# Sparse attention of one decoder layer: four head pairs written out, doubled buffers, the softmax division on GpSimd

## What is computed

```python
logits = jnp.einsum('bqhd,bqkhd->bhqk', q, k_sel).astype(jnp.float32) * (HEAD_DIM ** -0.5)
logits = jnp.where(valid[:, None], logits, -jnp.inf)
p = jax.nn.softmax(logits, axis=-1)
return jnp.einsum('bhqk,bqkhd->bqhd', p.astype(v.dtype), v_sel)
```

## Time and profile before

| | us |
|---|---|
| median of 3 runs (2573.61 to 2583.09) | 2574.93 |
| the profiled execution | 2575.35 |
| its span in the trace | 2573.7 |
| `sparse`, first q transpose to the last copy of o (1081.3 to 1255.6) | 174.3 |

### The profile page before, as it was taken

One profiled execution on the slowest core, in us unless ns is written; L12 is line 12 of the kernel. 1 busy time (PEld: TensorE's weight loads), 2 busy tenths in 40 slices (PEclk: granted clock), 3 DMA queues, 4 the chain that ended last, 5 costly groups with the idle time before them and its releaser, 6 DMA issues. The chain is left out here.

```text
span 2573.7 us, 37913 instructions
## 1 busy us (share of the span) xinstructions
PE 2251.4 (87%) x13113; PEld 1818.4 (71%) x13113; DVE 1382.0 (54%) x2547; ACT 804.6 (31%) x1357; POOL 138.7 (5%) x226
## 2 busy tenths in 40 slices
PE   4877799999997888788578789979999999999995
PEld 3823588888884445455346567869999999999994
DVE  4416878565563442275334454434566656665566
ACT  4026210211215656566333342212222122212212
POOL 0000000000002443200100000000000000000000
PEclk9988899999998989999789989989999999999998
DMA  3212123223212110211399962202111011101102
GB/s 129 78 34 52 61 84 113 82 82 114 82 47 57 36 35 15 56 37 53 84 312 388 349 199 107 99 5 65 50 49 46 27 49 49 49 25 49 49 16 85
DMA packets 187163, 218.57 MB, mean 85 GB/s; under 512 B 28924, under 2 KB 120956, under 8 KB 185916
## 3 DMA queue, kind: packets, MB, share of 16 engines
q1 hardware_dynamic: 178740, 214.03, 25.2%
q10 hardware_dynamic: 8072, 3.05, 0.6%
q0 software_dynamic: 256, 0.27, 0.1%
HBM read 181.17 MB, written 36.13 MB: 84 GB/s over the span
## 5 line engine op out<-in xcount | busy, mean ns | idle before, releaser
L2417 DVE TENSOR_TENSOR x_all<-x_all,ff_down 128x512 f32<-128x512 f32 x396 | 272.2, 687 | 163.4 <-PE ff_down L2321 158.7
L2306 PE MATMUL ff_up<-m_hi,ff_up_hi 128*128 128x368 f32 x1056 | 348.4, 330 | 7.5 <-DVE ff_up_lo L2394 7.5
L2307 PE MATMUL ff_up<-m_lo,ff_up_hi 128*128 128x368 f32 x1056 | 348.8, 330 | 0.0
L2308 PE MATMUL ff_up<-m_hi,ff_up_lo 128*128 128x368 f32 x1056 | 348.2, 330 | 0.0
L411 PE MATMUL pr_acc<-pr_w_hi,h_hi 128*128 128x512 f32 x720 | 281.5, 391 | 16.2 <-DVE pr_w_lo L352 16.2
L412 PE MATMUL pr_acc<-pr_w_lo,h_hi 128*128 128x512 f32 x720 | 281.2, 391 | 0.0
L413 PE MATMUL pr_acc<-pr_w_hi,h_lo 128*128 128x512 f32 x720 | 281.0, 390 | 0.0
L827 DVE TENSOR_SCALAR_CACHE_REDUCE bi_flags<-scores,bi_thr 128x384 bf16<-128x384 f32 (+6 forms) x252 | 235.5, 992 | 1.3
L2306 PEld LDWEIGHTS ff_up<-m_hi,ff_up_hi 128*128 128x128 f32 x1056 | 198.8, 188 | 8.8 <-DVE ff_up_lo L2394 7.9
L2307 PEld LDWEIGHTS ff_up<-m_lo,ff_up_hi 128*128 128x128 f32 x1056 | 198.9, 188 | 0.9
L2308 PEld LDWEIGHTS ff_up<-m_hi,ff_up_lo 128*128 128x128 f32 x1056 | 198.8, 188 | 0.0
(11 more groups left out here) (289 smaller groups left out, 3801.4 us busy)
## 6 DMA issues: line engine op xcount, KB each, us to landing
out_proj<-pr_staged SPq DMA_DIRECT2D x90, 256.0 KB, 2.0
up_raw<-in_w_up SPq DMA_DIRECT2D x44, 512.0 KB, 5.0
w_raw<-in_w_in SPq DMA_DIRECT2D x10, 2048.0 KB, 7.9
sa_keys<-in_cache_k_a SPq DMA_DIRECT2D x64, 256.0 KB, 4.2
sa_keys<-in_cache_k_b SPq DMA_DIRECT2D x64, 256.0 KB, 7.7
sa_values<-in_cache_v_a SPq DMA_DIRECT2D x64, 256.0 KB, 7.5
sa_values<-in_cache_v_b SPq DMA_DIRECT2D x64, 256.0 KB, 5.3
ff_down_raw<-in_w_down SPq DMA_DIRECT2D x22, 512.0 KB, 3.5
```

The lines of the kernel that those rows point to most:

```text
L2306: pe.matmul(up[n][:], w, hi[:, c, at], start=c == 0, stop=False)
L2307: pe.matmul(up[n][:], w, lo[:, c, at], start=False, stop=False)
L2308: ins = pe.matmul(up[n][:], w_rest, hi[:, c, at], start=False, stop=c == KC - 1)
L2417: dve.tensor_tensor(at, at, down[n][:], ALU.add).then_inc(down_added.sem, 1)
```

## The change

`sparse` is written anew, and everything else is left as it is.

- The loop over pairs is gone: the instructions of all four pairs are written out, and the pipeline runs over g = 0..35, the 36 tiles of all pairs. All waits are on constants.
- `q_t`, `k_t`, `v_rows` and `o_all` are doubled, `prob` and its small companions have four buffers instead of three.
- The q/k batches of pair i+1 are made while pair i runs: batches 0 and 1 in step t = 6, batches 2 and 3 in step 7, batch 4 in step 8 (`QK_WITH`). They share the ring of four banks with the scores.
- The lags grow: turn(g) runs in step g+3 instead of g+2, use(g) in step g+4 instead of g+3, the copy of o in g+5.
- The division's two multiplications move from DVE to GpSimd. The reciprocal stays on DVE.

```diff
-    NS, NTB, R = 4, 2, 3
+    NS, NTB, R, TURN_LAG, USE_LAG = 4, 2, 4, 3, 4
+    NG = PAIRS * NT
+    QK_WITH = {6: (0, 1), 7: (2, 3), 8: (4,)}
...
-    q_rows, k_rows, v_rows = sb("q_rows", [P, NT, P]), sb("k_rows", [P, NT, P]), sb("v_rows", [P, NT, P])
-    q_t, k_t = sb("q_t", [P, ROWS]), sb("k_t", [P, ROWS])
+    v_rows = [sb(f"v_rows{b}", [P, NT, P]) for b in range(2)]
+    q_t = [sb(f"q_t{b}", [P, ROWS]) for b in range(2)]
+    k_t = [sb(f"k_t{b}", [P, ROWS]) for b in range(2)]
...
+        @block.gpsimd
+        def _(pool):
+            for g in range(NG):
+                r, w = tile_rows(g % NT), key_width(g % NT)
+                pool.wait_ge(parted, g + 1)
+                for hh in range(2):
+                    x = prob[g % R][hh][0:r, 0:w]
+                    pool.tensor_scalar(x, x, part[g % R][0:r, hh:hh + 1], None, ALU.mult).then_inc(shared, 1)
...
+            for b in range(len(QK)):
+                turn_qk(0, b)
+            for n in range(NG + USE_LAG):
+                if n < NG:
+                    score(n)
+                    i, t = divmod(n, NT)
+                    for b in QK_WITH.get(t, ()) if i + 1 < PAIRS else ():
+                        turn_qk(i + 1, b)
+                if TURN_LAG <= n < NG + TURN_LAG:
+                    turn(n - TURN_LAG)
+                if n >= USE_LAG:
+                    use(n - USE_LAG)
...
+            for n in range(NG + TURN_LAG):
+                if n < NG:
+                    i, t = divmod(n, NT)
+                    for b in QK_WITH.get(t, ()) if i + 1 < PAIRS else ():
+                        take_qk(i + 1, b)
+                if 1 <= n <= NG:
+                    power(n - 1)
+                if n >= TURN_LAG:
+                    take_turns(n - TURN_LAG)
...
-                        for hh in range(2):
-                            x = prob[t % R][hh][0:r, 0:w]
-                            dve.tensor_scalar(x, x, part[t % R][0:r, hh:hh + 1], None, ALU.mult).then_inc(shared.sem, 1)
...
+            for n in range(NG + USE_LAG + 1):
+                if n < NG:
+                    mask(n)
+                if 1 <= n <= NG:
+                    invert(n - 1)
+                if n >= USE_LAG + 1:
+                    evacuate(n - USE_LAG - 1)
```

More of the change, by code:

```diff
@@ L1348, in turn, with turn_qk @@
-            def turn(i, t):
-                r = tile_rows(t)
-                for c in turns_of[t]:
+            def turn_qk(i, b):
+                what, t0, n = QK[b]
+                c = copies_of[i, b]
+                if b == 0:
+                    pe.wait_ge(qk_in, 32 * (i + 1))
+                wait_taken(pe, c - NS)
+                for t in range(t0, t0 + n):
+                    for k, rows in enumerate([q_rows, k_rows] if what == "both" else [q_rows if what == "q" else k_rows]):
+                        at = (t - t0 + k) * P
+                        ins = pe.transpose(banks[c % NS][:, at:at + P], rows[:, t, :], ident[:])
+                ins.then_inc(made, 1)
@@ new lines, in score @@
+            def score(g):
+                i, t = divmod(g, NT)
+                if t == 0:
+                    pe.wait_ge(qk_out, by_act[copies_of[i, len(QK) - 1]])
+                for c, hh, k, a, w in scores_of[g]:
+                    if hh == 0:
+                        wait_taken(pe, c - NS)
+                        wait_taken(pe, c + 1 - NS)
+                    pe.matmul(banks[c % NS][:, 0:w], q_t[i % 2][half(hh), t * P:(t + 1) * P],
+                              k_t[i % 2][half(hh), a:a + w], start=True, stop=True).then_inc(made, 1)
@@ new lines, in use @@
+                        ins = pe.matmul(o[g % 2][half(hh), 0:r], v_rows[i % 2][0:w, kt, half(hh)],
+                                        prob_t[g % 2][hh][0:w, kt, 0:r], start=kt == 0, stop=kt == t)
+                ins.then_inc(used, 1)
+            for b in range(len(QK)):
+                turn_qk(0, b)
[9 more added lines that the diff above has]
+                    use(n - USE_LAG)
@@ new lines, in invert, with evacuate @@
+            def invert(g):
+                r = tile_rows(g % NT)
+                dve.wait_ge(powered, 2 * g + 2)
+                if g >= R:
+                    dve.wait_ge(shared, 2 * (g - R + 1))
+                dve.reciprocal(part[g % R][0:r, :], total[g % R][0:r, :]).then_inc(parted, 1)
+            def evacuate(g):
+                i, t = divmod(g, NT)
+                dve.wait_ge(used, g + 1)
+                if t == 0 and i >= 2:
+                    dve.wait_ge(stored[i % 2], 16 * (i // 2))
+                r = tile_rows(t)
+                dve.tensor_copy(o_all[i % 2][:, t * P:t * P + r], o[g % 2][:, 0:r]).then_inc(o_out, 1)
```

264 lines of the change are left out of this document (115 added, 149 removed).

## The result

The changed kernel takes 2590.05 us, the median of five runs (2584.68 to 2593.09). The kernel before took 2574.93 us beside it, also five runs (2573.61 to 2583.09). The ratio is 1.0052, with a 95% interval of 1.0032 to 1.0073. On a second chip, against 11 runs of the kernel before, six more runs gave 1.0046 (1.0032 to 1.0059). So the change makes the kernel slower by about half a per cent: 12 to 13 us by the ratios, 15 us by the medians of the first measurement. The profiled execution is the one of 2590.05 us, 14.7 us above the profiled execution of before.

A forecast was written before the change was run, and what follows sets the result against it. PE was taken as the bound, busy 87% of the span, so only its 26.8 us of idle time in the stage could be won. 2575.35 + 3.4 (idle) + 3.5 (clock) gave 2582 us, range 2564 to 2596.

The forecast's parts named there:

- Idle time: PE's idle time in the stage: 24 us for three handovers plus 6.2 us elsewhere, 30.2 us against 26.8 before.
- steps 7, 8 and 9: Pipeline steps at each handover between pairs, where PE would stand still for 3.0, 3.0 and 1.35 us behind ACT.
- the small steps: Steps 3 to 5 of a pair, where tiles are small; 1 us of PE idle time was forecast there.
- ACT's chain of 4.6 us: In step 7, from batch 2's start on PE: two q/k copies 1.78, two exponentials 2.06, hand-off 0.74 us.
- the 0.93 us for two batches: PE's work on batches 2 and 3 in step 7, which with five transposes of 0.7 us fills part of the wait.
- The clock: PE's clock falls in every second of six stalls, 3 x 1.7 us, less 1.6 at the old seam: +3.5 us.
- The rival with a fall in every stall: The clock falls in every stall and stays low longer, 5 us, costing 2.5 us each: 2592 us; chance 0.20.
- The period: Time from pair to pair in the stage: about 44 us, against 42.6 before.
- GpSimd's price: The division's multiplications on GpSimd: 1.6 us for 1024 elements; up to 3.8 ns an element nothing waits, 0 in the sum.
- DVE's relief: The division leaves DVE, about 9 us less per pair, from 28 to some 19 us; alone worth little.
- DVE beside POOL: GpSimd's work holding up DVE's operations in the stage: 0 us.
- The covered rival: ACT finishes the exponential before PE's third group, handovers cost nothing, the stage falls to 156 us: 2557 us; chance 0.09.

The follow-up runs named there:

- e4_filler: The changed kernel with 16 repeated transposes in the second group of turn(4) and turn(5) of the first three pairs, filling PE's stalls; ratio 1.0045 to the kernel before.
- e1_act_order: The changed kernel with ACT's exponential of tile n-1 ahead of the q/k batch copies of step n; 2574.15 us, ratio 0.9984 to the kernel before.
- e2_div_vector: The changed kernel with the division's two multiplications back on DVE, right behind the reciprocal; ratio 1.0073 to the kernel before.
- e3_both: The changed kernel with the exponential ahead of the q/k copies on ACT and the division back on DVE; ratio 1.0003 to the kernel before.
- e10_between_div_vector: e8_use_between with the division back on DVE; ratio 0.9976 to the kernel before.
- e8_use_between: e1_act_order with PE's products of tile n-4 put between the second and third group of turn(n-3); 2561.91 us, ratio 0.9936 to the kernel before.
- e11_lag_two: e1_act_order with the short lags of before (turns 2 steps behind the scores, products 3), division on GpSimd; ratio 1.0060 to the kernel before.

## Why the prediction was right, and where it was wrong

The forecast was 2582 us; it came to 2590, inside the range. The direction was the forecast's and the size was not: 7 us slower were expected, 12 to 15 were measured.

- **Idle time: right.** 30.2 us forecast, 30.8 measured. For the stalls the counting gave 3.0, 3.0 and 1.35 us for steps 7, 8 and 9; they are 2.76, 2.71 and 1.00 in the first handover and 0.51 in the later ones. With the short waits around them a full period has 8.4 us, where 8 for the handover and a part of 1 us for the small steps were forecast. The step 9 value is 0.51 where the clock is low and 1.00 at full clock (e4_filler has 1.00 in all three). ACT's chain of 4.6 us came out at 4.57. PE's own work beside it is 1.81 us (1105.72 to 1107.53), not 1.63: the 0.93 us for two batches does not follow from the rows named for it, whose 0.50 and 0.66 give 1.16 us, and with that the stall would have come to 2.7 us. e1_act_order shows that the cause is the one named, two q/k copies and two exponentials ahead of the group's copy.
- **The clock: the step that failed.** "I take a fall in every second one, 3 x 1.7 = 5.1 us, less 1.6" gave +3.5 us. The profiled execution has +8.4 us of clock loss (13.4 against 5.0), the second one +4.3. Part of this is the start of the stage, which the term was not about: 4.1 and 1.5 us there, 3.3 in the kernel before. Behind the start the loss is 9.3 and 7.9 us, where the term had 5.1, against 1.7 before, where it had 1.6: +7.6 and +6.2 us in place of +3.5. There were falls at four of the six stalls in the first profile and at five in the second, and in the first another without a long stall (1185), so five falls in each. Nine of the ten lost 1.4 to 1.7 us, as taken, and one of 7 us lost 3.0. So what was low is above all the number of falls, five where the term had three. The rival with a fall in every stall (2592) is nearer to the measured 2590 than the forecast, though most of its falls would be too long. In timed runs the filler moved 2 us at most, so how much of the missing 5 to 8 us is the clock's on average stays open.
- **The period** was to be 44 us and is 46 to 49. PE's 36 us at full clock (e1's period has that) and 8.4 us of idle time are 44.4, and e4_filler, with the same pipeline, took 44.99 us where its clock didn't fall; the other 1.0 to 4.0 us are the clock again.
- **GpSimd's price: wrong in size, right in effect.** 1.6 us for 1024 elements were taken and 2.84 us measured, 2.8 ns an element, above the 2.45 of the two-operand row and far from the copy's. The 132 us of work lie between the bounds of 70 and 183. Since 2.8 ns are under the 3.8 at which it decides, nobody waits for it (0.7 us), and the sum had 0, as measured.
- **DVE's relief: undervalued.** "Worth little", the prediction said; e2_div_vector, e3_both and e10_between_div_vector put it at 5 to 10 us. The idle forecast was counted with a light DVE, so the sum didn't suffer, but a reader who took the change apart by the text would have kept the wrong half.
- **DVE beside POOL: right.** The masks of 128x512 take 688 ns on average beside POOL's multiplications and took 685 before.
- **The covered rival**, 2557 us with a stage of 156, is no fantasy: e8_use_between has a stage of 158.3 and, by its ratio, 2558.5 us on the scale of the first measurement. What decided against it in the change is the order on ACT, as written.

DVE's masks of 512 in the kernel before and in the changed one, and POOL's multiplications by form:

```profile
L1452 DVE CUSTOM_DVE_ANT_0 sp_prob<-sp_dots,masks 128x512 f32<-128x512 f32 x48 | 30.8, 685 | 2.9 <-PE sp_dots L1345 2.9
```
```profile
L1484 DVE CUSTOM_DVE_ANT_0 sp_prob<-sp_banks,masks 128x512 f32<-128x512 f32 x48 | 30.9, 688 | 20.1 <-PE sp_banks L1382 19.8
```
```profile
L1358 POOL TENSOR_SCALAR sp_prob<-sp_prob,sp_part 128x1024 f32<-128x1024 f32 x8 | 22.7, 2843 | 15.0 <-DVE sp_part L1498 15.0
...
L1358 POOL TENSOR_SCALAR sp_prob<-sp_prob,sp_part 128x128 f32<-128x128 f32 x8 | 4.7, 594 | 24.4 <-DVE sp_part L1498 24.4
```

## What to carry to other kernels

When a loop is written out so that the next iteration's work overlaps this one's, look at the place of each new piece in every in-order list, and not only at the amount of work: here a copy that must first wait for another engine, set ahead of an exponential that is ready, cost more than the seam it removed, and swapping the two gave 17 us. Take the change apart, too: with that order right, the overlap alone gave no time over the kernel before (e3_both), and the gain came from the division on GpSimd. Look for the bank with the tightest reuse and put ready work between its two uses; here that was worth another 12 us. A slow engine is a good home for work whose result is needed late: lengthen the lag first, then move it. With the short lag the kernel was 20 us slower than with the long one (e11_lag_two against e1_act_order), and the same move in the kernel before cost 42 us.

## What the runs showed of the hardware

- A multiplication by a scalar for each partition takes 2843 ns on GpSimd for 1024 float32 elements and 594 for 128, so over this range 2.5 ns an element and 0.27 us beside it. DVE took 749 ns and 283 ns. The Trainium skill, "GPSIMD Engine Reference", section "When to use GPSIMD", has one-input work at roughly line rate; here it is 3.8 times slower than DVE at 1024, and the measurement decides. Its advice to leave elementwise work on VectorE would have cost 5 us here.
- TensorE's granted clock fell to its lower level after stalls of 2.7 us in four and in five of six cases, and among many waits of at most 1.7 us too (e11_lag_two, five falls behind the start of the stage). In the kernel before, where PE waits at most 1.2 us at a time in the stage, it fell at 1091 and at 1176; in e1_act_order, where it waits at most 1.4 us, it did not fall again after the stage's start. Two profiles of the same kernel with identical stalls had it at partly different places and 13.4 and 9.3 us in sum. A difference in clock between two single profiles is no measurement of its price.
- The time outside the stage, which no kernel here changes, lies between 2399.5 us (e11_lag_two: 2590.79 - 191.3) and 2408.1 us (e3_both: 2581.73 - 173.6) in the profiled executions, so a single one can't tell a few us apart; the stage itself can.
